# A two-layer GLA and Mamba-2 decoder step: scan outputs made by channels instead of by tokens

## The chip, the cores and the metric
One core of one Trainium2 chip runs the whole program. Five engines work in parallel, each through its own instructions in order: TensorE (PE, its weight loads shown as PEld), VectorE (DVE), ScalarE (ACT), GpSimd (POOL) and SyncE (SP), which issues most DMAs. The metric is the device time of one launch in microseconds, the median of three runs; less is better.

## The reference
Two layers over 1048 tokens: 8 samples of one token each, 16 meta tokens and 1024 prompt tokens. Layer 0 mixes by gated linear attention (GLA, 4 heads), layer 1 by Mamba-2 SSD (32 heads in 4 groups).
```python
for i in range(DEPTH):                       # x <- x + post(mixer(pre(x)))
    h = rmsnorm(x, pre_norm[i])
    y, S = gla_mixer(...) if i == 0 else ssd_mixer(...)
    x = x + rmsnorm(y, post_norm[i])
# GLA, per chunk
o = einsum('bhij,bjhv->bihv', attn, v) + einsum('bihk,bhkv->bihv', q * exp(bcum), S)
S = exp(b_last)[..., None] * S + einsum('bjhk,bjhv->bhkv', k_dec, v)
# then: o * rsqrt(mean(o*o) + EPS) * w_norm * silu(r), times w_out
# SSD, per chunk
y = einsum('bijg,bijgr,bjgrp->bigrp', cb, lmat * dt[:, None], x)
y = y + einsum('bign,bgrpn->bigrp', Cm, S) * exp(acum)[..., None]
S = exp(a_last)[..., None, None] * S + einsum('bjgn,bjgr,bjgrp->bgrpn', Bm, w, x)
# then: y + d_skip * x, times silu(z); rmsnorm over each group's 512 channels; times w_out
```

## The kernel before
Tokens are cut in 9 steps: step 0 has 24 tokens (samples and meta), steps 1 to 8 have 128 each. They form two groups (steps 0 to 4, steps 5 to 8), and the channels four units (a GLA head or an SSD group). An event is one unit at one step: 36 events per layer, 32 of 128 tokens.

The projection of a unit (L1257) is cut in pieces, 128 output channels by 268 or 512 tokens, each 24 products of fp32r high and low parts (weights w made by ACT L733 and DVE L747 from w_raw). It leaves channels in partitions and stores them to DRAM (kept_gq, kept_sq). The scan reads a chunk back per event: g_chunk (q, k, cumulative gate, v, v, r, r) or s_chunk (x in 4 tiles, B, C), and for the SSD s_decay (cumulative decay of 8 heads, laid over all partitions) and s_z (gate, 4 tiles).

`Plan` writes one order for all engines: `skeleton` lists an event's stages by name with an offset in events, and between them ("fill", x) lets in x shares of projection pieces, so that PE has work while the other engines prepare an event. Every engine runs its part of each stage in that order. When the last unit's projection is through, the fills are empty, and the last events of layer 1 stand bare. All products of plain f32 operands run as two records.

A GLA event: PE turns v and r (4 transposes, L1636), ACT copies them to vr_turned (L1648). PE makes the score levels (L1695, L1698, L1701), DVE merges them to g_attn (L1716). PE adds q x state (L1775, 128 tokens by 256 channels) and attention x v (L1792) in bank O, and makes the state's increment (L1776). DVE gates with r (L1799), ACT squares with a sum (L1810), POOL takes the root, PE turns o (2 transposes, L1818), ACT and DVE make its high and low parts (L1827, L1835), and PE multiplies by w_out (L718, helper `out_products`). ACT or DVE (L1882) scale by the root and add to y_acc.

An SSD event: PE turns x and B and multiplies B by C (L2066 to L2068). ACT makes decays (L2039 to L2051), DVE the masked and scaled operands (L2094 to L2108). `pe_scan`: C x state (L2191, one product of 512 columns in bank Y1), the state's increment (L2194 in bank SU), and for each of 8 heads the product inside the chunk (L2201: stationary decay 128x128, moving xdt of 64 columns). DVE updates the state and sums y (L2212 to L2234). PE turns z (4 transposes, L2243) into bank SU and DVE gates y by it (L2250). ACT squares with a sum (L2259); PE turns y (L2267) into SU; ACT makes s_yt_hi (L2276), DVE s_yt_lo (L2282); PE makes the output product (L718). As SU serves the state's increment and both turns, L2191's stage first waits until s_yt_lo is made (`banks_free`).

In step 0 each of the 8 samples has a state of its own. In the GLA each is multiplied by a stationary operand of 24 columns that is zero but for one (q_masked, L1742); in the SSD PE turns the sample's state (L2138), ACT copies it to s_ys (L2159), and L2148 multiplies it by c_masked in the same way, 512 columns wide; L2144 makes its increment.

Two lines that the words above rest on (L2191 and L2201):
```python
pe.matmul(self.Y[1][0:n, :], x[:, 5, :], self.S[:, u % 2, :], start=True, stop=True).then_inc(self.inter, 1)
last = pe.matmul(self.Y[0][0:n, r * HD:(r + 1) * HD], G[0:n, r, :], t["xdt"][0:n, r * HD:(r + 1) * HD],
                 start=True, stop=True)
```

## Time and profile before
| | us |
|---|---|
| three runs, median (lowest, highest) | 1708.35 (1705.63, 1716.34) |
| the profiled execution, its own time | 1704.04 |
| its span, first to last instruction | 1702.3 |
| PE busy | 1586.8 |
| DVE busy | 1212.3 |
| ACT busy | 805.9 |

The profile is of one execution, and numbers worked out from it are held against its own 1704.04 us, 4.3 us under the median. Busy times of PE overlap, as matmuls are pipelined; the distance between the starts of two rows of the timeline, divided by the first one's count, is its pace.

### The profile page before, as it was taken

The page shows a single profiled execution, that of the slowest core. Times are in us where ns is not written, and L with a number is a line of the kernel's source. Part 1 is how long each engine was busy: PE and PEld are TensorE (multiplying, and loading weights), DVE is VectorE, ACT ScalarE, POOL GpSimd, SP SyncE. Part 2 cuts the span into 40 slices and gives each one's busy share as a digit, 9 for nine tenths or more (in the row PEclk, how much of TensorE's full clock was granted, in tenths as well). Part 3 has the DMA queues.
Part 4 walks back from the last instruction along what each step waited for, and adds up shares of the span by engine and source line. Part 5 has one row for each costly group of instructions (what it writes and reads, how often), then busy time and mean ns, then how long its engine had stood idle before and what let it go on. Part 6 is the DMA issues. An engine that isn't in the chain of part 4 may idle for free. (4 is left out here: it accounts for less than half of the span.)

```text
span 1702.3 us, 26480 instructions
## 1 busy us (share of the span) xinstructions
PE 1586.8 (93%) x9274; PEld 1298.3 (76%) x9274; DVE 1212.3 (71%) x2351; ACT 805.9 (47%) x1738; POOL 228.7 (13%) x412
## 2 busy tenths in 40 slices
PE   6999999899999889979999999999999999999885
PEld 6879787667878778976788887787577778878764
DVE  4455487767877978867677678785677878587675
ACT  4634343355446454443553544444345455454451
POOL 4010112011211100112002002200201200000012
PEclk9999999999999999988999999999899999999998
DMA  5553446245565314455735564652465766665652
GB/s 166 149 153 108 134 137 173 62 122 161 159 208 172 111 47 124 147 162 172 176 91 155 160 165 136 185 133 65 144 173 144 196 175 158 162 159 134 165 128 80
DMA packets 313531, 244.80 MB, mean 144 GB/s; under 512 B 32773, under 2 KB 283465, under 8 KB 313369
## 3 DMA queue, kind: packets, MB, share of 16 engines
q1 hardware_dynamic: 305400, 216.90, 46.9%
q0 software_dynamic: 8000, 26.22, 5.0%
q8 instruction: 75, 1.23, 0.3%
q14 instruction: 56, 0.45, 0.1%
HBM read 182.59 MB, written 60.68 MB: 143 GB/s over the span
## 5 line engine op out<-in xcount | busy, mean ns | idle before, releaser
L1257 PE MATMUL bank<-h,w 128*128 128x268 f32 (+1 forms) x4752 | 841.8, 331 | 18.2 <-ACT w L733 15.7
L1257 PEld LDWEIGHTS bank<-h,w 128*128 128x128 f32 x4752 | 701.3, 191 | 122.5 <-issue 56.1
L718 PE MATMUL bank<-s_w_out,s_yt_hi 128*128 128x512 f32 (+1 forms) x576 | 182.7, 398 | 7.4 <-DVE s_ys L2234 3.2
L747 DVE TENSOR_TENSOR w<-w_raw,w 128x1024 fp32r<-128x1024 f32 x132 | 160.8, 1218 | 37.6 <-ACT w L733 37.3
L733 ACT ACTIVATE w<-w_raw 128x1024 fp32r<-128x1024 f32 x132 | 138.8, 1052 | 24.6 <-DMA w_raw<-in_ssd_w_in_dram 24.2
L1346 DVE SCALAR_TENSOR_TENSOR conv<-before_conv,cw,conv 128x260 f32<-128x260 f32 (+2 forms) x216 | 125.1, 579 | 6.8
L718 PEld LDWEIGHTS bank<-s_w_out,s_yt_hi 128*128 128x128 f32 (+1 forms) x576 | 101.0, 180 | 36.1 <-issue 4.4
L718 PE MATMUL bank<-s_w_out,s_yt_lo 128*128 128x512 f32 (+1 forms) x288 | 113.6, 394 | 0.0
L2019 POOL TENSOR_SCALAR s_ymean<-s_ysum 128x1 f32<-128x1 f32 (+1 forms) x36 | 17.2, 478 | 678.4 <-ACT squares L2259 678.4
L718 PE MATMUL bank<-g_w_out,g_ot_hi 128*128 128x512 f32 (+1 forms) x288 | 100.1, 430 | 1.9 <-DVE g_ot_lo L1835 1.9
L2044 ACT ACTIVATE s_decay<-s_decay,t_ac 128x128 f32<-128x128 f32 (+1 forms) x288 | 85.4, 378 | 1.2
L1716 DVE COPY_PREDICATED g_attn<-g_lmask,bank 128x128 f32<-128x128 int32 (+1 forms) x208 | 60.7, 292 | 29.4 <-PE bank L1698 21.3
L2201 PEld LDWEIGHTS bank<-s_xdt,s_decay 128*128 128x128 f32 (+1 forms) x576 | 66.8, 183 | 19.4 <-issue 19.4
L1301 ACT ACTIVATE conv<-bank,cw 128x268 f32<-128x268 f32 (+1 forms) x72 | 45.9, 638 | 72.1 <-PE bank L1257 65.8
L1558 POOL TENSOR_SCALAR g_omean<-g_osum 128x1 f32<-128x1 f32 (+1 forms) x36 | 16.2, 451 | 432.3 <-ACT squares L1810 432.3
L1386 DVE SCALAR_TENSOR_TENSOR stage<-stage,conv 128x268 f32<-128x268 f32 (+1 forms) x72 | 37.2, 517 | 48.1 <-ACT stage L1363 47.7
L2276 ACT ACTIVATE s_yt_hi<-bank 128x512 fp32r<-128x512 f32 (+1 forms) x36 | 20.1, 558 | 107.5 <-PE bank L2267 107.4
L718 PEld LDWEIGHTS bank<-g_w_out,g_ot_hi 128*128 128x128 f32 (+1 forms) x288 | 53.1, 187 | 19.4 <-DVE g_ot_lo L1835 4.0
L2201 PE MATMUL bank<-s_xdt,s_decay 128*128 128x64 f32 (+1 forms) x576 | 65.6, 267 | 0.0
L749 DVE SCALAR_TENSOR_TENSOR s_w_out<-w_raw,wn,s_w_out 128x1024 fp32r<-128x1024 f32 x32 | 40.9, 1281 | 32.6 <-ACT s_w_out L740 32.6
L740 ACT ACTIVATE s_w_out<-w_raw,wn 128x1024 fp32r<-128x1024 f32 x32 | 36.7, 1146 | 56.3 <-DMA w_raw<-in_ssd_w_out_dram 29.2
L718 PEld LDWEIGHTS bank<-s_w_out,s_yt_lo 128*128 128x128 f32 (+1 forms) x288 | 51.6, 179 | 15.0
(213 smaller groups left out, 2560.9 us busy)
## 6 DMA issues: line engine op xcount, KB each, us to landing
w_raw<-in_ssd_w_in_dram SPq DMA_DIRECT2D x80, 512.0 KB, 4.2
w_raw<-in_gla_w_in_dram SPq DMA_DIRECT2D x48, 512.0 KB, 4.3
s_decay<-kept_acd SPq DMA_DIRECT2D x32, 512.0 KB, 8.1
w_raw<-in_ssd_w_out_dram SPq DMA_DIRECT2D x32, 512.0 KB, 4.0
g_chunk<-kept_gq SPq DMA_DIRECT2D x32, 448.0 KB, 5.0
s_chunk<-kept_sq SPq DMA_DIRECT2D x32, 384.0 KB, 4.4
kept_sq<-stage SPq DMA_DIRECT2D x80, 134.0 KB, 4.4
kept_sq<-stage SPq DMA_DIRECT2D x40, 256.0 KB, 4.9
```

What stands on the lines that cost most here:

```text
L718: last = pe.matmul(bank[0:n, :], yt[a][:, k, 0:n], wo[:, k, b, 512 * half:512 * half + 512], start=(k + a + b == 0), stop=(k == tiles - 1 ...
L733: act.activation(self.part(i, 0), self.raw(i), ACT.Copy).then_inc(self.w_hi, 1)
L740: act.activation(self.part(i, 0), self.raw(i), ACT.Copy, scale=self.norm_column(w)).then_inc(self.w_hi, 1)
L747: dve.tensor_tensor(self.part(i, 1), self.raw(i), hi, ALU.subtract).then_inc(self.w_lo, 1)
L749: dve.scalar_tensor_tensor(out=self.part(i, 1), in0=self.raw(i), scalar=self.norm_column(w), in1=hi, op0=ALU.mult, op1=ALU.subtract).then_ ...
L1257: last = pe.matmul(bank[:, 0:n], w[:, p.tile % 2, a, k, :], h[:, b, k, c:c + n], start=(i == 0), stop=(i == len(terms) - 1))
L1301: act.activation(self.work(i)[:, 0:n], bank[:, 0:n], ACT.Identity, scale=m["cw"][:, 3, a:a + 1], bias=m["cw"][:, 4, a:a + 1])
L1346: ins = dve.scalar_tensor_tensor(out=u[:, off:n], in0=x[:, k:k + w], scalar=cw[:, k, a:a + 1], in1=u[:, off:n], op0=ALU.mult, op1=ALU.add)
L1386: dve.scalar_tensor_tensor(out=self.slot(i)[:, 0:n], in0=self.slot(i)[:, 0:n], scalar=1.0, in1=self.work(i)[:, 0:n], op0=ALU.add, op1=ALU. ...
L1716: dve.copy_predicated(g[:, :], mk[:, li, :].bitcast(I32), self.L[li // 4][0:n, (li % 4) * P:(li % 4) * P + n]).then_inc(self.attn_part, 1)
L2044: last = act.activation(L[0:n, r, :], L[0:n, r, :], ACT.Relu, scale=-1.0, bias=ac[0:n, s, h:h + 1])
L2201: last = pe.matmul(self.Y[0][0:n, r * HD:(r + 1) * HD], G[0:n, r, :], t["xdt"][0:n, r * HD:(r + 1) * HD], start=True, stop=True)
```

## The change
Both scans make their outputs with channels in partitions and tokens along the row, as the output product wants them.

In the SSD, C x state becomes 4 products (stationary a 128x128 piece of the state, moving C). The product inside the chunk has xdt (64 columns) as stationary and the decay matrix (128 columns) as moving operand, and writes even heads to partitions 0 to 63 and odd heads to 64 to 127. Skip, gate and halving read s_chunk and s_z as they lie; exp of the running sum is taken per head over all tokens (e_sum is now 4 tiles of 128). The turns of z and y are gone. ACT squares y in place once its low part is made; PE sums the squares over channels by 4 products with a column of ones (`pe_sum`, stage "sum"), ACT copies that column (`act_sum`, stage "root"), POOL takes the root as before.

In the GLA v alone is turned, r is used as it lies, q x state and attention x v are two products each of 128 channels, o is not turned, and its squares are summed in the same way. The state lies in states after even steps and in odd_state after odd ones. The chunk has three buffers instead of two.

Samples: the state (SSD: the turned one) is the stationary operand in pieces of 128, the sample's q or C the moving one, a single column; q_masked and c_masked are gone. Their GLA outputs are added by DVE in two small instructions per unit. s_z and conv_rows have one buffer instead of two; s_z is loaded by a stage of its own ("zload"), and conv_rows are stored one piece earlier.
```diff
         gla = [... ("turn", -1), ("fill", 0.5), ("load", 2),
-               ("fill", 0.5), ("samples", 0.4), ("state", 0), ("fill", 0.5), ("attend", 0), ("scale", 1),
+               ("sum", -1), ("fill", 0.5), ("root", -1), ("samples", 0.4), ("state", 0), ("fill", 0.5), ("attend", 0),
@@ ssd
-               ("weight", 3, 1), ("fill", 0.5), ("gates", 0), ("load", 2), ("lows",), ("fill", 0.3), ("norm", 0),
+               ("weight", 3, 1), ("fill", 0.5), ("load", 2), ("lows",), ("fill", 0.3), ("norm", 0), ("zload", 1),
...
-               ("fill", 0.3), ("lows",), ("weight", 2, 0), ("fill", 0.3), ("r_square", -1), ("r_out", -2), ("fill", 0.3)]
+               ("fill", 0.3), ("lows",), ("square", 0), ("weight", 2, 0), ("fill", 0.3), ("sum", 0), ("r_square", -1),
+               ("r_out", -2), ("fill", 0.3), ("root", 0)]
@@ Gla.pe_attend (state product moved here from pe_state)
+        for j in range(2):
+            out = self.O[:, j * P:j * P + n]
+            if s:
+                pe.matmul(out, self.state(u, s - 1)[:, j * P:(j + 1) * P], self.t["qe"][:, e % 2, 0:n], start=True,
+                          stop=False)
+            if j == 0:
+                pe.wait_ge(self.attn, e + 1)
+            last = pe.matmul(out, v[:, j * P:(j + 1) * P], g[:, :], start=(s == 0), stop=True)
@@ Ssd.load_gate, act_decay
+        if e:
+            sp.wait_ge(self.gated, e)
+        for i in range(2):
+            half = slice(HD * i, HD * i + HD)
+            act.activation(t["ea"][half, e % 2, :, 0:n], L[half].rearrange("p (t two) c -> p t two c", two=2)[:, :, i, :],
+                           ACT.Exp)
@@ Ssd.banks_free, pe_scan
-            pe.wait_ge(self.yt_lo, e)
-            pe.matmul(self.Y[1][0:n, :], x[:, 5, :], self.S[:, u % 2, :], start=True, stop=True).then_inc(self.inter, 1)
+            for j in range(4):
+                last = pe.matmul(self.Y[1][:, j * P:j * P + n], self.S[:, u % 2, j * P:(j + 1) * P], x[:, 5, :],
+                                 start=True, stop=True)
         for r in range(HPG):
-            last = pe.matmul(self.Y[0][0:n, r * HD:(r + 1) * HD], G[0:n, r, :], t["xdt"][0:n, r * HD:(r + 1) * HD],
+            at = slice(HD * (r % 2), HD * (r % 2) + HD)
+            last = pe.matmul(self.Y[0][at, (r // 2) * P:(r // 2) * P + n], t["xdt"][0:n, r * HD:(r + 1) * HD], G[0:n, r, :],
                              start=True, stop=True)
@@ Ssd: squares, sum and its copy
+        act.wait_ge(self.yt_lo, e + 1)
+        act.activation(y, y, ACT.Square).then_inc(self.rows.squared, 1)
+    def pe_sum(self, pe, u, s):
+        pe.wait_ge(self.rows.squared, self.rows.squares[("square", 1, u, s)])
+        pe.wait_ge(self.cb_masked, min(e + 2, len(EVENTS)))
+        for j in range(4):
+            last = pe.matmul(self.M[0:n, 2 * P:2 * P + 1], self.t["y"][:, j, 0:n], self.m["ones"][:, 0:1],
+                             start=(j == 0), stop=(j == 3))
+    def act_sum(self, act, u, s):
+        act.activation(self.t["ysum"][0:n, e % 4:e % 4 + 1], self.M[0:n, 2 * P:2 * P + 1],
+                       ACT.Copy).then_inc(self.sum_kept, 1)
```
PE, from the output product of one SSD event of group 1 to the next event's scan, before (ident is the unit matrix of a transpose, h,w a projection piece; the waits are semaphores by name):
```order
L2267 MATMUL bank<-ident,s_ys 128x128 [waits s_s_new,s_gated]
L2267 MATMUL bank<-ident,s_ys 128x128 x3
L1234 MATMUL bank<-ident,conv_cols 11x128 [waits piece_packed,piece_free0]
L1234 MATMUL bank<-ident,conv_cols 11x128
L1257 MATMUL bank<-h,w 128x512 [waits w_hi,piece_free1]
L1257 MATMUL bank<-h,w 128x512 x15
L1257 MATMUL bank<-h,w 128x512 [waits w_lo]
L1257 MATMUL bank<-h,w 128x512
L2191 MATMUL bank<-states,s_chunk 128x512 [waits s_s_new,s_yt_lo,s_y_summed,s_added]
L2194 MATMUL bank<-s_xw,s_b_turned 128x512 [waits s_b_turned,s_xw_ready]
L2201 MATMUL bank<-s_xdt,s_decay 128x64 [waits s_attn]
L2201 MATMUL bank<-s_xdt,s_decay 128x64 x7
```
And in the changed kernel:
```order
L1269 MATMUL bank<-h,w 128x512 x7
L1246 MATMUL bank<-ident,conv_cols 11x128 [waits piece_packed,piece_free0]
L1246 MATMUL bank<-ident,conv_cols 11x128
L1269 MATMUL bank<-h,w 128x512 [waits w_hi,piece_free1]
L1269 MATMUL bank<-h,w 128x512 x11
L2314 MATMUL bank<-ones,s_ys 128x1 [waits s_cb_masked,row_squared]
L2314 MATMUL bank<-ones,s_ys 128x1 x3
L1269 MATMUL bank<-h,w 128x512 x4
L1269 MATMUL bank<-h,w 128x512 [waits w_lo]
L1269 MATMUL bank<-h,w 128x512
L2233 MATMUL bank<-s_chunk,states 128x128 [waits s_s_new,s_y_summed,s_added]
L2233 MATMUL bank<-s_chunk,states 128x128 x3
```
The turns L2267 are gone, the sum L2314 stands some 12 projection products later and waits for the squares, and the state product, now L2233, no longer waits for s_yt_lo. Ahead of the first row stand 10 and 1 further projection products behind the output product in both.

PE in a GLA event of group 0, from the turn of o to the output product, before:
```order
L1818 MATMUL bank<-ident,g_o_gated 128x128 [waits g_vr_turned,g_o_gated]
L1818 MATMUL bank<-ident,g_o_gated 128x128
L1257 MATMUL bank<-h,w 128x268 x6
L1257 MATMUL bank<-h,w 128x268 [waits w_hi,piece_free0]
L1257 MATMUL bank<-h,w 128x268 x11
L1775 MATMUL bank<-states,g_q_inter 128x256 [waits row_squared,g_k_turned,g_o_gated,g_s_new,g_vr_turned,g_qi_ready]
L1776 MATMUL bank<-g_vr_turned,g_k_turned 128x256
L1257 MATMUL bank<-h,w 128x268 x4
L1257 MATMUL bank<-h,w 128x268 [waits w_lo]
L1257 MATMUL bank<-h,w 128x268
L1792 MATMUL bank<-g_vr_turned,g_attn 128x256 [waits g_attn]
```
And in the changed kernel:
```order
L1269 MATMUL bank<-h,w 128x268 x6
L1851 MATMUL bank<-ones,g_o_squares 128x1 [waits g_v_turned,row_squared]
L1851 MATMUL bank<-ones,g_o_squares 128x1
L1269 MATMUL bank<-h,w 128x268 x6
L1269 MATMUL bank<-h,w 128x268 [waits w_hi,piece_free1]
L1269 MATMUL bank<-h,w 128x268 x5
L1792 MATMUL bank<-g_v_turned,g_k_turned 128x256 [waits g_s_new,g_k_turned,g_v_turned]
L1269 MATMUL bank<-h,w 128x268 x6
L1815 MATMUL bank<-g_q_inter,g_odd_state 128x128 [waits g_o_gated,row_squared,g_v_turned,g_qi_ready]
L1819 MATMUL bank<-g_attn,g_v_turned 128x128 [waits g_attn]
L1815 MATMUL bank<-g_q_inter,g_odd_state 128x128
L1819 MATMUL bank<-g_attn,g_v_turned 128x128
```
The sum L1851 has come in behind six projection products, the two turns have gone, and q x state has moved from the state stage to the attention stage and is cut in two.

PE in the last unit of layer 1, where no pieces are left, before (from the end of an output product):
```order
L718 MATMUL bank<-s_w_out,s_yt_lo 128x512
L2267 MATMUL bank<-ident,s_ys 128x128 [waits s_s_new,s_gated]
L2267 MATMUL bank<-ident,s_ys 128x128 x3
L2191 MATMUL bank<-states,s_chunk 128x512 [waits s_s_new,s_yt_lo,s_y_summed,s_added]
L2194 MATMUL bank<-s_xw,s_b_turned 128x512 [waits s_b_turned,s_xw_ready]
L2201 MATMUL bank<-s_xdt,s_decay 128x64 [waits s_attn]
L2201 MATMUL bank<-s_xdt,s_decay 128x64 x7
L2243 MATMUL bank<-ident,s_z 128x128 [waits s_s_new,s_z_in1]
L2243 MATMUL bank<-ident,s_z 128x128 x3
L2066 MATMUL bank<-ident,s_chunk 128x128 [waits s_cb_masked,s_skipped,s_ck_in0]
```
And in the changed kernel:
```order
L724 MATMUL bank<-s_w_out,s_yt_lo 128x512
L2314 MATMUL bank<-ones,s_ys 128x1 [waits s_cb_masked,row_squared]
L2314 MATMUL bank<-ones,s_ys 128x1 x3
L2233 MATMUL bank<-s_chunk,states 128x128 [waits s_s_new,s_y_summed,s_added]
L2233 MATMUL bank<-s_chunk,states 128x128 x3
L2238 MATMUL bank<-s_xw,s_b_turned 128x512 [waits s_b_turned,s_xw_ready]
L2246 MATMUL bank<-s_decay,s_xdt 64x128 [waits s_attn]
L2246 MATMUL bank<-s_decay,s_xdt 64x128 x7
L2111 MATMUL bank<-ident,s_chunk 128x128 [waits s_cb_masked,s_sum_kept,s_xdt_ready,s_ck_in1]
```
The sum now stands directly behind the output product and ahead of the next event's scan.

## Rows read from the trace of the kernel before
**Rows 1.** The page's parts 1 and 2: busy time per engine; clock in 40 slices
```profile
PE 1586.8 (93%) x9274; PEld 1298.3 (76%) x9274; DVE 1212.3 (71%) x2351; ACT 805.9 (47%) x1738; POOL 228.7 (13%) x412
...
PEclk9999999999999999988999999999899999999998
```
**Rows 2.** Waits of PE up to 1550 us: us in total, times, longest
```profile
PE bank L1257 <- ACT w L733: 14.5, 9, 2.7
...
PE bank L2191 <- DVE s_yt_lo L2282: 4.6, 3, 3.8
PE bank L2243 <- DVE states L2216: 3.4, 3, 1.7
```
**Rows 3.** Waits of PE behind 1550 us
```profile
PE bank L2191 <- DVE s_yt_lo L2282: 7.9, 5, 2.9
PE bank L718 <- DVE s_ys L2234: 3.2, 4, 1.9
```
**Rows 4.** Timeline of PE, an event of the last unit: start us, us, what
```profile
1611.42 1.02 PE L2194 MATMUL bank<-s_xw,s_b_turned 128*128 128x512 f32 x2
1612.28 1.89 PE L2201 MATMUL bank<-s_xdt,s_decay 128*128 128x64 f32 x16
1614.01 0.61 PE L2243 MATMUL bank<-ident,s_z 128*128 128x128 f32 x4
1614.45 0.60 PE L2066 MATMUL bank<-ident,s_chunk 128*128 128x128 f32 x4
...
1615.84 0.70 PE L718 MATMUL bank<-s_w_out,s_yt_hi 128*128 128x512 f32 x2 [0.45 <-DVE s_ys L2234]
```
**Rows 5.** Timeline of PE, state products of a GLA event
```profile
506.59 0.59 PE L1775 MATMUL bank<-states,g_q_inter 128*128 128x256 f32 x2
507.02 0.59 PE L1776 MATMUL bank<-g_vr_turned,g_k_turned 128*128 128x256 f32 x2
```
**Rows 6.** Timeline of PE, levels of a GLA event
```profile
501.50 0.27 PE L1664 MATMUL bank<-ident,g_decays 128*128 128x128 f32 x1
501.70 0.51 PE L1695 MATMUL bank<-g_q_decayed,g_decays 128*64 128x64 f32 x6
502.14 1.38 PE L1698 MATMUL bank<-g_q_decayed,g_decays 128*128 128x128 f32 x10
503.36 0.39 PE L1701 MATMUL bank<-g_chunk 128*128 128x128 f32 x2
```
**Rows 7.** Groups of instructions by form: busy us, mean ns
```profile
L1257 PE MATMUL bank<-h,w 128*128 128x512 f32 x1584 | 403.1, 404 | 11.8 <-ACT w L733 11.8
...
L1108 PE MATMUL bank<-t_esum,ident 32*64 32x8 f32 x64 | 3.6, 250 | 0.0
...
L1695 PEld LDWEIGHTS bank<-g_q_decayed,g_decays 128*32 128x32 f32 x128 | 4.6, 108 | 2.2
...
L1882 DVE SCALAR_TENSOR_TENSOR y_acc<-bank,s_yrstd,y_acc 128x512 f32<-128x512 f32 x48 | 35.3, 746 | 29.5 <-PE bank L718 29.4
...
L2282 DVE TENSOR_TENSOR s_yt_lo<-bank,s_yt_hi 128x512 fp32r<-128x512 f32 x32 | 22.0, 688 | 17.1 <-ACT s_yt_hi L2276 17.0
...
L2276 ACT ACTIVATE s_yt_hi<-bank 128x512 fp32r<-128x512 f32 x32 | 19.1, 597 | 104.4 <-PE bank L2267 104.3
...
L2039 ACT ACTIVATE s_e_sum<-t_ac 128x8 f32<-128x8 f32 x32 | 6.4, 201 | 12.4 <-DMA s_decay<-kept_acd 12.4
```
**Rows 8.** Timeline of PE's weight loads, narrow stretch in rows 6
```profile
501.96 0.14 PEld L1695 LDWEIGHTS bank<-g_q_decayed,g_decays 128*32 128x32 f32 x4
```
**Rows 9.** Timeline of PE, one sample in the SSD
```profile
1051.45 1.04 PE L2148 MATMUL bank<-s_ys,s_c_masked 128*24 128x512 f32 x2
1052.42 1.74 PE L1257 MATMUL bank<-h,w 128*128 128x268 f32 x12
```
**Rows 10.** Windows: the last samples' stretch; busy us by engine, clock
```profile
1190.00:1206.00 16.00, 12.15 (x48) 8.18 (x46) 12.20 (x24) 4.32 (x9) 3.07 (x4) 0.68 0.48 152
```

More of the change, by code:

```diff
@@ L488, in _ @@
                 rows.root(pool, ("r", *at))
[L489 removed]
+            elif name == "root":
                 layers[at[0]].root(pool, *at[1:])
@@ L526, in _ @@
                 layers[at[0]].act_square(act, *at[1:])
+            elif name == "root":
+                layers[at[0]].act_sum(act, *at[1:])
             elif name == "turn":
@@ L596, in _ @@
                 ssd.pe_scan(pe, *at[1:])
-            elif name == "gates":
-                ssd.pe_gates(pe, *at[1:])
             elif name == "sample":
                 layers[at[0]].pe_sample(pe, *at[1:])
-            elif name == "turn":
-                layers[at[0]].pe_turn(pe, *at[1:])
+            elif name == "sum":
+                layers[at[0]].pe_sum(pe, *at[1:])
             elif name == "products":
@@ L1282, in act_evac @@
         elif p.kind == "tail":
-            if p.u or p.j == 2:
-                act.wait_ge(self.cv_stored, 128 * p.u + (64 if p.j == 2 else 0))
-            act.activation(m["cvo"][:, p.j % 2, :], bank[0:11, 0:2 * P], ACT.Copy).then_inc(self.free[i % 3], 1)
+            if p.u or p.j:
+                act.wait_ge(self.cv_stored, 128 * p.u + 32 * p.j)
+            act.activation(m["cvo"][:, :], bank[0:11, 0:2 * P], ACT.Copy).then_inc(self.free[i % 3], 1)
         elif p.kind == "plain":
@@ L1554, in root @@
         q = slice(e % 4, e % 4 + 1)
-        pool.wait_ge(self.rows.squared, self.rows.squares[("square", 0, u, s)])
+        pool.wait_ge(self.sum_kept, e + 1)
         if e >= 4:
@@ L1762, in dve_sample, with state @@
                                      op0=ALU.mult, op1=ALU.add).then_inc(self.ss_new, 1)
+    def state(self, u, s):
+        return self.t["odd"][:, :] if s % 2 else self.S[:, u, :]
     def pe_state(self, pe, u, s):
@@ L1797, in dve_gate @@
         if e:
-            dve.wait_ge(self.o_turned, e)
-        dve.tensor_tensor(t["og"][0:n, :], self.O[0:n, 0:HV], t["vr"][0:n, e % 2, HV:2 * HV],
+            dve.wait_ge(self.ot_hi, e)
+            dve.wait_ge(self.ot_lo, e)
+        if s == 0:
+            samples, own = self.output(NS), self.O[:, 2 * P:2 * P + 2 * NS].rearrange("p (t c) -> p t c", t=2)
+            dve.tensor_copy(t["os"][:, :, :], own).then_inc(self.with_states, 1)
+            dve.wait_ge(self.with_states, 2 * u + 1)
+            dve.tensor_tensor(samples, samples, t["os"][:, :, :], ALU.add).then_inc(self.with_states, 1)
+            dve.wait_ge(self.with_states, 2 * u + 2)
+        dve.tensor_tensor(t["og"][:, :, 0:n], self.output(n), self.tokens(u, s)[:, 5:7, :],
                           ALU.mult).then_inc(self.o_gated, 1)
@@ L2014, in root @@
         q = slice(e % 4, e % 4 + 1)
-        pool.wait_ge(self.rows.squared, self.rows.squares[("square", 1, u, s)])
+        pool.wait_ge(self.sum_kept, e + 1)
         if e >= 4:
@@ L2038, in act_decay @@
             act.wait_ge(self.y_summed, e - 1)
-        act.activation(t["ea"][0:n, e % 2, :], ac[0:n, s, HPG * u:HPG * u + HPG], ACT.Exp)
+        for i in range(2):
+            half = slice(HD * i, HD * i + HD)
+            act.activation(t["ea"][half, e % 2, :, 0:n], L[half].rearrange("p (t two) c -> p t two c", two=2)[:, :, i, :],
+                           ACT.Exp)
         act.activation(t["el"][:, e % 2, :].unsqueeze(2), L[:, :, n - 1:n], ACT.Exp).then_inc(self.el_done, 1)
@@ L2147, in pe_sample @@
         pe.wait_ge(self.ss_copied, i + 1)
-        pe.matmul(self.Y[1][0:n, :], t["cm"][:, b * C0:(b + 1) * C0], t["y"][:, :], start=(b == 0),
-                  stop=(b == NS - 1)).then_inc(self.inter if b == NS - 1 else self.ss_inter, 1)
+        for j in range(4):
+            last = pe.matmul(self.Y[1][:, j * P + b:j * P + b + 1], t["y"][:, j, :],
+                             self.tokens(u, 0)[:, 5, b:b + 1], start=True, stop=True)
+        last.then_inc(self.inter if b == NS - 1 else self.ss_inter, 1)
     def act_sample(self, act, u, b):
@@ L2153, in act_sample @@
         if b == 0 and e:
-            act.wait_ge(self.y_turned, e)
-            act.wait_ge(self.rows.squared, self.rows.squares[("square", 1, *EVENTS[e - 1])])
+            act.wait_ge(self.sum_done, e)
         act.wait_ge(self.ss_turned, NS * u + b + 1)
@@ L2172, in dve_sample, with tiles @@
             self.mask_b(dve, i + 1)
+    def tiles(self, bank, n):
+        return bank[:, :].rearrange("p (t c) -> p t c", t=4)[:, :, 0:n]
     def banks_free(self, pe, e):
@@ L2238, in pe_gates, with dve_gate @@
-    def pe_gates(self, pe, u, s):
+        dve.tensor_tensor(y[:, :, 0:c], y[:, :, 0:c], old, ALU.add).then_inc(self.y_summed, 1)
+    def dve_gate(self, dve, u, s):
         e, n = ev(u, s), step_cols(s)[1]
-        pe.wait_ge(self.z_in[e % 2], 16 * (e // 2 + 1))
-        pe.wait_ge(self.s_new, e + 1)
-        for j in range(4):
-            last = pe.transpose(self.SU[0:n, j * P:(j + 1) * P], self.t["zc"][:, e % 2, j, 0:n], self.m["ident"][:, :])
-        last.then_inc(self.z_turned, 1)
-    def dve_gate(self, dve, u, s):
-        e, n, y = ev(u, s), step_cols(s)[1], self.t["y"]
-        dve.wait_ge(self.z_turned, e + 1)
+        y = self.t["y"][:, :, 0:n]
+        dve.wait_ge(self.z_in, 16 * (e + 1))
```

275 lines of the change are left out of this document (134 added, 141 removed).

## The prediction
> **What bounds the kernel now.** I read the page first: TensorE (PE) is busy 93% of the span and VectorE (DVE) 71%, and the clock row stands at 9 in nearly every slice [rows 1]. So a microsecond taken off PE's work should come off the time, unless PE is standing there for somebody else. Second, PE's waits. They are short and scattered; those that bear on the change are 4.6 us before the state product L2191, for s_yt_lo, and 3.4 us before the turns of z, for the state, both up to 1550 us [rows 2]. Behind 1550 us the picture differs: there 7.9 us are waited in five stands for s_yt_lo, and 3.2 us for y itself [rows 3]. The program has run out of projection products there, and six events of the last unit stand bare. Third, the timeline, for the pace of PE. A busy time on PE overlaps its neighbours, so I take the distance from one start to the next, divided by the count.
>
> **The pace of PE.** An f32 product comes as two records, a transpose as one. Four transposes of 128x128 take 1614.01 to 1614.45, 0.11 us each [rows 4]. Two records of 512 columns take 0.86 us, 0.43 each [rows 4]; two of 256 take 0.43, 0.215 each [rows 5]; ten of 128 take 1.22, 0.12 each with a change of form among them [rows 6]. Sixteen records of only 64 columns (L2201) take 1.73 us, 0.108 each [rows 4]. That row is the key to this case: half the columns cost no less than all of them, so a record with a stationary operand 128 wide costs 0.11 us by its weight load, whatever it multiplies. A stationary operand of 64 with 8 columns has 3.6 us for 64 records, 0.056 [rows 7], again half for half the width.
>
> **The change part by part (PE's work).** An event is one unit's step; 36 per layer, 32 of 128 tokens and 4 of 24.
>
> Turns removed: z 144, y 144, o 72, r 72 transposes. Where 128 wide and long (384 of them) 0.11 each, the 24 of y's and o's that carry 24 tokens some 0.08, the 24 of z and r 0.11: 47 us less.
>
> Sums by a column of ones: per event 4 products in the SSD and 2 in the GLA, two records each, stationary 128 wide, one column. 384 full records at 0.11 are 42.2 us, 48 of 24 tokens at some 0.03 by their width are 1.4: 43.7 us more. So the turns that go are paid for almost wholly by the products that come. From below, at 0.056 a record, they are 22 us; from above 0.12 each, 47 us. I take 0.11, by the row of 64 columns.
>
> State and attention outputs cut in pieces of 128 columns: GLA 128 records of 0.215 (27.5 us) become 256 of 0.11 (28.2); SSD state products 64 of 0.43 (27.5) become 256 of 0.11 (28.2). 1.4 us more.
>
> The product inside the chunk (L2201, now L2246) swaps its operands: stationary 64 wide, moving 128, outputs in turns in partitions 0 to 63 and 64 to 127. If such neighbours run one behind the other, 16 records cost 16 x 0.11 = 1.76 us and two changes of form. The price of a change: from a transpose to L1695 0.20 us instead of 0.11, and six small records with a change inside take 0.44 us where by their widths (two at 0.056, four at 0.028) they would take 0.22 [rows 6], so 0.1 to 0.14 a change; two are 0.28. If the two halves run side by side, 8 x 0.11 + 0.28 = 1.16 us. The trace has such a pair: the four loads of the 32-wide forms of L1695, which go to two column groups, all start within 0.03 us and are over in 0.14 us, where a lone one takes 0.11 [rows 7, 8]. I take side by side: 1.73 less 1.16, 0.57 us less in each of 32 events, 18.2 us. The other end is 0.31 us more, 10 us more. The Trainium skill (TensorEngine Tiling, Key Properties) says both things: tiles in different columns load and multiply in parallel, and a change of tiling mode drains the engine. Of 64-wide pairs no run here shows it; the 32-wide pair of this trace agrees, with 0.14 us for four loads.
>
> Sample states: in the SSD the two records of 24x512 per sample take 0.97 us (1051.45 to 1052.42) [rows 9] and become 8 of one column at 0.11, 0.90; the form then changes once less, as the transposes before it and these products are both 128 wide: 0.12. 32 samples: 6 us less. In the GLA 64 records of 256 (13.8 us) become 128 of one column (14.1), and 16 changes of form go (1.9): 1.6 less.
>
> Sum of PE's work: -47.0 + 43.7 + 1.4 - 18.2 - 7.6 = -27.7 us.
>
> **Waits.** (a) The state product no longer waits for s_yt_lo, as y isn't turned in its bank, and the z turns that waited are gone: 4.6 + 3.4 = 8 us less up to 1550 us [rows 2]. What is late next there are the squares, but in 21 events PE has 4 to 8 us of work between the output product and the sum (counted in the changed order; in the place that the change's order rows show, 30 products of 512 columns at 0.25 [rows 7]), and the chain that has to fit is 2.6 us, so they are covered.
> (b) That chain: the output product ends, DVE adds its second half to y_acc (0.75), then y_lo (0.69), ACT squares (0.6, as its 128x512 copy), with three hops of some 0.15 [rows 7]: 2.6 us, in place of the waits before L2191 of 7.9/5 = 1.6 us [rows 3]. In the six bare events PE has nothing to cover it: 1.0 x 6 = 6 us more.
> (c) In the same six the gain on z and inside the chunk isn't had: the next output product waits for y_summed, which DVE ends after six operations in a row; PE already stands there, 3.2 us in four events [rows 3], and at 1615.84 it starts behind DVE, not behind its own work [rows 4]. 6 x (0.44 + 0.57) = 6 us given back.
> (d) Eight further events have only 1.4 to 2.8 us of products before the sum: some 0.3 us each, 2 us. The last event of each layer now has sum, copy and root behind the turn: 1 us each, 2 us.
> (e) ScalarE gets 36 x about 1.0 us: exp of the running sum is taken for all 128 tokens of 4 tiles by two instructions (64x512, each about 0.6 by the 128x512 row) in place of one of 0.20 [rows 7]. They stand one event ahead of need. What they can hurt are weights: PE waits 14.5 us for them today [rows 2]. I take 2 us; the bounds are 0 and 36.
> (f) The z load has one buffer and waits for the gate of the event before; SP issues it behind that gate and DVE is mostly its pacer, the load lands within an event of some 20 us: 0. conv_rows with one buffer: ACT waits for the store of the piece before, a few us off the path: 0 to 4, taken 0. VectorE loses some 8 us of narrower work in the four short events of each layer and is hidden: 0.
>
> Sum of waits: -8 + 6 + 6 + 2 + 2 + 2 = +10 us. All: -17.7, say -18. The profiled execution has 1704.04 us (its span 1702.3), so 1686; the median of the three runs lies 4.3 above it, so 1690.
>
> **Rivals.**
> 1. No side by side: the 64-wide halves take turns. 0.88 us more than forecast in the 26 events that aren't bare, 23: 1713. For it: the trace shows only 32-wide pairs. Against: [rows 8].
> 2. A one-column product hides its load and costs 0.056: 384 records of the sums and 384 of the samples at 0.054 less each, 41 us, 1649. For it: the 8-column row [rows 7]; against it: the 64-column row [rows 4], with the same width of load. The Trainium skill (TensorEngine Tiling, Instruction Overhead) gives about 60 cycles to any small product and tells nothing of the load; by it alone the sums and one-column products would cost even less than this rival's. The trace speaks against it with 0.108 us for 64 columns.
> 3. Slower: the chain to the sum becomes what PE waits for in every SSD event, not in the bare ones only, because ACT, now 1 us fuller per event, comes late to the squares, and PE stands in its order before the sum with the next state product behind it. Decides from the point at which the squares come more than the covering 4 to 8 us after the output product. With 2 us each in the 30 other events: 60 more, 1750; with half of it 1720. For: ACT and DVE take their work in a fixed order, and DVE is 71% busy. Against: ScalarE is 47% busy [rows 1], 36 us more make it 49%.
>
> **How the numbers follow.** Forecast as it stands, within 10 us: 0.47. Rival 1: 0.13. Rival 2: 0.06. Rival 3: 0.07. Rival 4: 0.08. Rival 5: 0.19. A measurement here can tell about 1% from no change, 17 us: below 1691 is faster, above 1725 slower. The forecast lies at that edge, so half of its share counts as faster (0.25), with rivals 2 and 5: 0.50 (rounded); slower 0.07 from rival 3 and 0.03 from 1 and 4 together: 0.10; the rest, 0.40, within 1%. Range 1664 to 1716: down beyond rival 5, up to 1 and the milder half of 4.
>
> **What would show it.** Records of L2246 in eight pairs, 1.1 to 1.3 us an event, not 1.9; sum products (L2314, L1851) at 0.11 a record; PE busy down by some 28 us; a wait of PE before L2314 of some 2.5 us in six events behind 1550 and none to speak of before; the wait before the output product in those six grown by about 1 us; ScalarE up by some 35 us. I am wrong if PE's work falls by less than 15 or by over 45 us, if L2314 waits in the middle of the layer, or if the time moves while PE's work doesn't.

## The result, and the profile after

The changed kernel is slower: 1798.32 us (median of four, 1794.35 to 1803.35) against 1712.34 (1705.63 to 1716.46) of the kernel before beside it, a ratio of 1.051 with a 95% interval of 1.0482 to 1.0539. The forecast was 1690, range 1664 to 1716. Here and below a median takes in every execution, while a ratio leaves out those in the slow state that some executions of any kernel show (a lower granted clock and a longer time).

The page after, where [rows 1] stands for the kernel before, and below it the line with the span and the mean granted clock:
```profile
PE 1647.2 (92%) x9858; PEld 1389.6 (78%) x9858; DVE 1205.1 (67%) x2350; ACT 838.8 (47%) x1776; POOL 215.0 (12%) x411
...
PEclk9999796989999998979997998999999999989987
```
```profile
core 0: 1792.6 us, clock 0.926
```
PE's busy time didn't fall by 28 us, it rose by 60. Its share of the span is still 92%, so by the busy shares nothing happened but more work. The clock row tells more: it had 9 nearly everywhere and now dips all along. TensorE's clock is granted at one of two levels, 2.4 and 1.2 GHz, so a mean of 0.926 over 1792.6 us is 2 x 0.074 x 1792.6 = 265 us at half clock. The kernel before had a mean of 0.976, 82 us by the same working. I call this the half-clock time.

On PE's side the 90 us by which the span grew are of two kinds. All its waits together are 101 us before and 131 after, 30 more (forecast: 10 more). The other 60 are busy time. As an estimate, if work takes twice as long at half clock, the 183 us of additional half-clock time cost some 92, so that the work at full clock fell by some 32, about as forecast (28).

PE's waits after (us in total, times, longest), which answer to [rows 2, 3]:
```profile
PE bank L2314 <- ACT s_ys L2307: 57.5, 30, 4.1
...
PE bank L1269 <- ACT w L739: 9.5, 6, 3.2
...
PE bank L724 <- DVE s_ys L2279: 5.7, 5, 1.7
```
The waits for s_yt_lo are gone, as forecast. In their place PE stands ahead of the SSD's sum of squares (L2314) in 30 events of 36, and this is now the longest wait by far. It splits into the events up to 1680 us, which have other products ahead of the sum, and the six bare ones behind 1680 us:
```profile
PE bank L2314 <- ACT s_ys L2307: 42.8, 24, 4.1
```
```profile
PE bank L2314 <- ACT s_ys L2307: 14.7, 6, 3.9
```
The event with the longest of these waits, in the timeline of all engines (start us, us, what, and in brackets the idle time and who ended it):
```profile
1057.45 4.60 PE L1269 MATMUL bank<-h,w 128*128 128x268 f32 x36
...
1058.19 1.22 DVE L2151 TENSOR_TENSOR s_decay<-s_decay,s_cb 128x1024 f32<-128x1024 f32 x1
...
1059.14 0.57 ACT L1313 ACTIVATE conv<-bank,cw 128x268 f32<-128x268 f32 x1 [4.92 <-PE bank L1269]
...
1059.94 0.44 ACT L1375 ACTIVATE stage<-conv 128x268 f32<-128x268 f32 x1
1060.26 0.64 ACT L2295 ACTIVATE s_yt_hi<-s_ys 128x512 fp32r<-128x512 f32 x1
1060.64 1.22 DVE L753 TENSOR_TENSOR w<-w_raw,w 128x1024 fp32r<-128x1024 f32 x1
...
1063.26 1.54 DVE L1358 SCALAR_TENSOR_TENSOR conv<-before_conv,cw,conv 128x260 f32<-128x260 f32 x3
1064.71 0.68 DVE L2300 TENSOR_TENSOR s_yt_lo<-s_ys,s_yt_hi 128x512 fp32r<-128x512 f32 x1
1065.43 0.63 ACT L2307 ACTIVATE s_ys<-s_ys 128x512 f32<-128x512 f32 x1 [4.53 <-DVE s_yt_lo L2300]
1066.11 1.14 PEld L2314 LDWEIGHTS bank<-ones,s_ys 128*128 128x128 f32 x5 [4.27 <-ACT s_ys L2307]
1066.11 1.23 PE L2314 MATMUL bank<-ones,s_ys 128*128 128x1 f32 x5 [4.06 <-ACT s_ys L2307]
```
Three engines come in turn. The output product is over at 1057.6, where the projection products (L1269) take over. On ACT, y_hi (L2295) stands in order behind four instructions of a piece, the first of which waited for PE until 1059.14, so it starts at 1060.26; y_lo (L2300) starts at 1064.71 behind pieces' work on DVE; the square (L2307) writes over y in place, so it has to wait for y_lo, which reads y. From the end of the output product to the sum it is 8.5 us, and PE had 4.6 us of projection products for it. In the other 23 of the 24 events the wait is shorter, 1.8 us in the mean of all, but of the same kind: the sum comes 2.2 to 12.4 us after the last output product's end (later still in the layer's first event, which has none just before it).

The other half of the story is in the GLA, where no such wait is. The first 40 us of a unit with samples, before and after (window, its length, busy us and records of PE, PEld, DVE, ACT, POOL, then granted clock, DMA share, GB/s):
```profile
180.00:220.00 40.00, 35.53 (x221) 26.62 (x220) 21.08 (x47) 13.90 (x27) 7.35 (x12) 1.00 0.51 156
```
```profile
180.00:220.00 40.00, 39.08 (x214) 33.16 (x213) 15.40 (x31) 10.11 (x19) 6.62 (x10) 0.74 0.33 101
```
PE is busier than before in it, and gets through fewer records (214, not 221), at a clock of 0.74 instead of 1.00. With 4.5 us of idle time in this stretch the kernel before kept its full clock, and with 0.9 us the changed one lost it.

What came as forecast is the product inside the chunk. In the timeline of PE after:
```profile
1340.18 1.09 PE L2246 MATMUL bank<-s_decay,s_xdt 128*64 128x128 f32 x16
1341.20 1.43 PE L1269 MATMUL bank<-h,w 128*128 128x512 f32 x5
```
Sixteen records take 1.02 us from start to start, against 1.73 in [rows 4].

### The profile page after: what moved, and what is told of

It is laid out like the page before. It is cut to its first block and busy times, and to the rows that moved or that the text cites. A ratio compares the mean times of both kernels' runs of the same rounds, so it can differ in the third digit from the quotient of the medians.

```text
span 1792.6 us, 27581 instructions
## 1 busy us (share of the span) xinstructions
PE 1647.2 (92%) x9858; PEld 1389.6 (78%) x9858; DVE 1205.1 (67%) x2350; ACT 838.8 (47%) x1776; POOL 215.0 (12%) x411
## 5 line engine op out<-in xcount | busy, mean ns | idle before, releaser
L1269 PE MATMUL bank<-h,w 128*128 128x268 f32 (+1 forms) x4752 | 871.4, 338 | 14.1 <-ACT w L739 9.5
L1269 PEld LDWEIGHTS bank<-h,w 128*128 128x128 f32 x4752 | 723.3, 197 | 100.3 <-issue 31.0
L2314 PE MATMUL bank<-ones,s_ys 128*128 128x1 f32 (+1 forms) x288 | 39.2, 257 | 57.5 <-ACT s_ys L2307 57.5
L2314 PEld LDWEIGHTS bank<-ones,s_ys 128*128 128x128 f32 (+1 forms) x288 | 37.2, 203 | 68.5 <-ACT s_ys L2307 67.9
L1922 DVE SCALAR_TENSOR_TENSOR y_acc<-bank,s_yrstd,y_acc 128x512 f32<-128x512 f32 (+1 forms) x54 | 39.7, 745 | 42.1 <-PE bank L724 42.1
L2256 DVE TENSOR_TENSOR states<-states,s_e_last 128x512 f32<-128x512 f32 x32 | 22.1, 691 | 67.6 <-PE bank L2233 67.5
L2197 ACT ACTIVATE s_ys<-bank 128x512 f32<-128x512 f32 x32 | 19.1, 597 | 100.7 <-PE bank L2175 100.7
```

The lines of the kernel that those rows point to most:

```text
L1269: last = pe.matmul(bank[:, 0:n], w[:, p.tile % 2, a, k, :], h[:, b, k, c:c + n], start=(i == 0), stop=(i == len(terms) - 1))
L1922: return dve.scalar_tensor_tensor(out=y, in0=bank, scalar=rstd, in1=y, op0=ALU.mult, op1=ALU.add)
L2314: last = pe.matmul(self.M[0:n, 2 * P:2 * P + 1], self.t["y"][:, j, 0:n], self.m["ones"][:, 0:1], start=(j == 0), stop=(j == 3))
```

## The experiments

Two theories stood at the start. The chain theory: PE waits for the squares, 57.5 us, and this is the loss. The clock theory: the products of one column (samples' states and sums) go with a fall of the granted clock, and this is the loss. All ratios are to the kernel before, which ran beside each run; "less than the changed kernel" is the difference of two such ratios, times 1710 us. "The right version" is the changed kernel with all three of the following edits and every output kept.

**Wide samples.** In both layers, and alike for the GLA's L1755:
```diff
-            last = pe.matmul(self.Y[1][:, j * P + b:j * P + b + 1], t["y"][:, j, :],
-                             self.tokens(u, 0)[:, 5, b:b + 1], start=True, stop=True)
+            last = pe.matmul(self.Y[1][:, j * P:(j + 1) * P], t["y"][:, j, :],
+                             ident[:, :], start=True, stop=True)
```

> The changed kernel, but each of the samples' state products (64 of GLA at L1755, 128 of SSD at L2186) moves 128 columns of the identity instead of one column; the weights, the count, the order and the waits stay (the samples' outputs are no longer the reference's). Chain theory (TensorE stands for ACT's squares ahead of 30 of the 36 SSD sums, 57.5 us in all; the clock is a consequence): nothing at the samples, the wait L2314 <- ACT s_ys stays at 55 to 60 us and the time within 5 us of 1798. If both hold, the samples give 30 to 45 us and the wait stays.

Measured: 1750.38 us, ratio 1.0251 (1.0213 to 1.0289), 44 us less than the changed kernel by the ratios. Mean clock 0.955, half-clock time 157 us, 108 less. The window from 180 to 220 us again, then the wait:
```profile
180.00:220.00 40.00, 35.51 (x228) 28.70 (x227) 22.71 (x51) 12.68 (x24) 7.34 (x12) 0.93 0.47 144
```
```profile
PE bank L2314 <- ACT s_ys L2307: 56.9, 30, 4.0
```
The products have 128 times the columns, and the stretch has most of its clock back and gets through more records. The wait is untouched. PE's waits in all stay too (131 and 129 us in the two profiles), and its busy time falls by 45. So the samples' products of one column cost 44 us by the clock, apart from the wait. In the two profiles 23 us of the gain lie in layer 0 (up to the first scan product of layer 1) and 25 in layer 1.

**Wide sums.** `self.M[0:n, 2 * P:3 * P]` with `ones[:, :]` in place of one column, and alike in the GLA.

> The changed kernel, but the sums of squares (L1851, L2314) move 128 columns of ones instead of one, and the first column is read: same results, same count, order and waits. If the cost of the sums is that they leave the array idle (clock theory, taken to its end): some 10 to 20 us less, above all behind 1400 us where half-clock stretches stand once in an event. If their cost is the stationary load, 0.11 us a record whatever moves (47 us in all), and the stand ahead of them (chain theory): no change, 0 to +10 us, and the wait at L2314 stays at 55 to 60 us.

Measured: 1775.63 us, ratio 1.0386 (1.034 to 1.0431), 21 us less; mean clock 0.946. This is at the upper end of the clock theory's figure, and the wait at L2314 stays (57.8 us). All of it is in layer 1: layer 0 took 771.8 us in the changed kernel's profile and 771.5 here.

**Squares apart.** The squares go to the tile that the row norms use, ahead of y_hi on ACT. As y is no longer overwritten, DVE and ACT may also write the next event's y once y_lo and the squares are made, where they waited for PE's sum before:
```diff
-        act.wait_ge(self.yt_lo, e + 1)
-        act.activation(y, y, ACT.Square).then_inc(self.rows.squared, 1)
+        act.wait_ge(self.gated, e + 1)
...
+        act.activation(self.tiles(self.m["junk"], n), self.t["y"][:, :, 0:n], ACT.Square).then_inc(self.rows.squared, 1)
```

> The changed kernel, but SSD's squares go to a tile of their own (the one that the row norms use for theirs), straight from the gated output and ahead of y_hi on ACT, so that they wait for neither y_hi nor y_lo; the sum stays where it is on TensorE. Chain theory: the wait of L2314 for ACT falls from 57.5 us to under 15, and the time by 35 to 60 us, to 1740 to 1765. Clock theory alone: the stands are filled by other stands and the time stays within 10 us of 1798; half-clock time of the samples' steps stays (GLA about 90 us). If both hold: -35 or more and the GLA part unchanged.

Measured: 1740.79 us, ratio 1.0155 (1.0098 to 1.0211), 61 us less. PE's longest wait is now another:
```profile
PE bank L1276 <- ACT w L740: 25.0, 13, 3.2
```
The wait at the sum is 1.8 us, and that for the weights, which ACT makes, was 9.5 us and is 25.0: 15 us have moved there. All of PE's waits together fell from 131 to 106 us only. That the time fell by about the whole 57.5 nonetheless is the clock's doing: PE's busy time fell by 26 us as well (1647.2 to 1621.3), and half-clock time by 53. The figure that the chain theory had was hit, but only half of it as time waited; the other half is work that ran at half clock before.

**All three.**

> All three edits together (wide samples' products, wide sums, squares apart and early). If chain and clock are separate causes that add, 70 to 100 us less than the changed kernel: 1700 to 1730. If only the chain counts: 1740 to 1765; if only the clock: 1755 to 1770.

(As in the first run, the samples' products move the unit matrix and not their q or C.) Measured: 1693.19 us, ratio 0.9912 (0.9883 to 0.9941), 102 us less than the changed kernel. The single gains sum to 126, so 24 us were counted twice. The single edits took 108, 75 and 53 us off the half-clock time, 236 in all, and together they take 160: a wait that goes and a product that widens save partly the same half-clock time. Its mean clock is 0.969.

**All three, with every result right.** Widening can keep every output. NM is 16; the 16 columns from the sample's own on are moved seven times over, and later samples overwrite the columns beyond it:
```diff
+            at = j * P + b
+            last = pe.matmul(self.Y[1][:, at:at + 7 * NM].rearrange("p (r c) -> p r c", r=7), t["y"][:, j, :],
+                             self.tokens(u, 0)[:, 5, b:b + NM].unsqueeze(1).to_broadcast([P, 7, NM]),
+                             start=True, stop=True)
```

> All three edits with every result kept: the samples' state products move 112 columns (the 16 columns from the sample's own on, seven times over) of which the first is kept, the sums move 128 columns of ones, SSD's squares are apart and early. Same count of records as the changed kernel. If the width alone is what counted in the two runs with wide products, the time is that of the run with all three edits, 1693 within 8 us, and below the kernel before (1708.6); if it was that a constant was moved instead of each sample's column (another tile read), 1740 as with squares apart alone.

Measured: 1697.53 us, ratio 0.9932 (0.9915 to 0.995). This beats both kernels: 5.5% under the changed one, and 0.7% under the one before, which is small but outside the interval. Its page:
```profile
PE 1575.8 (93%) x9858; PEld 1334.7 (79%) x9858; DVE 1204.1 (71%) x2350; ACT 835.8 (49%) x1776; POOL 219.1 (13%) x411
```
```profile
core 0: 1696.4 us, clock 0.971
```
As many records of PE as the changed kernel, each with as many columns or more, and 71 us less busy time.

**Before, with narrow products.** The clock theory from the other side: in the kernel before, L1742 and L2148 move one column instead of 256 and 512 (so the samples' outputs lack their states' part). Their stationary tile is 24 columns wide.
```diff
-        pe.matmul(self.Y[1][0:n, :], t["cm"][:, b * C0:(b + 1) * C0], t["y"][:, :], start=(b == 0),
+        pe.matmul(self.Y[1][0:n, 0:1], t["cm"][:, b * C0:(b + 1) * C0], t["y"][:, 0:1], start=(b == 0),
```

> The kernel before, with its samples' state products (GLA L1742, 256 columns moved; SSD L2148, 512) cut to one moving column (the samples' state outputs are left out). Work alone: L1742's 15.6 us and L2148's 33.5 us fall to about 7 us each, so 33 to 36 us less: 1672 to 1677. Clock theory (one-column products let the granted clock fall): half-clock time in the steps with samples rises above that of before, and at least a third of this is given back: 1685 to 1710.

Measured: 1704.71 us, ratio 0.9975 (0.9956 to 0.9993). By form, the product in the SSD (busy us, mean ns), in the kernel before and then in this one, and this one's clock and window:
```profile
L2148 PE MATMUL bank<-s_ys,s_c_masked 128*24 128x512 f32 x64 | 35.7, 642 | 5.6 <-ACT s_ys L2159 5.5
```
```profile
L2148 PE MATMUL bank<-s_ys,s_c_masked 128*24 128x1 f32 x64 | 6.8, 175 | 7.6 <-ACT s_ys L2159 7.4
```
```profile
core 0: 1702.4 us, clock 0.955
```
```profile
180.00:220.00 40.00, 34.30 (x178) 26.21 (x178) 19.19 (x46) 11.07 (x20) 6.63 (x10) 0.79 0.48 143
```
From start to start, L2148 went from 33.5 to 4.6 us and L1742 from 15.6 to 4.3, 40 us of work on the engine that is busy 93%. The time fell by 4. Half-clock time rose from 82 to 153 us, and in the window the clock went from 1.00 to 0.79 with no other edit. Not all of the 36 us between was the clock: PE's waits in all rose from 101 to 115 us, some 14. The rest went into the products around, which took longer (the projection products alone 13 us, waits left out). Layer 0 shows the clock best. It lost 11 us of products and got 13 us longer (749.2 to 762.4), with 5 us more of waits and half-clock time up from 27 to 82. Layer 1 lost 29 us of products and got 13 us shorter.

**Sums of one record.** As the right version, but with float32r squares and ones.

> As the run with all three edits and right results, but the squares are written and the ones kept as float32r, so that each sum is one record instead of two (216 instead of 432), 64 columns wide. If a record of a sum costs TensorE 0.11 us by its stationary load whatever else (so the sums' 47 us are a true price), 20 to 26 us less than that run: about 1670. If it is the chain or the clock that fills, 0 to 10 less.

Measured: 1700.01 us, ratio 0.9925 (0.9896 to 0.9955), so nothing was gained on the right version. Its sums by form, and its clock:
```profile
L2333 PE MATMUL bank<-round_ones,squares 128*128 128x64 f32 x128 | 17.5, 260 | 2.0 <-issue 2.0
```
```profile
core 0: 1700.4 us, clock 0.960
```
The records did halve, and from start to start the sums fell from 48 to 24 us. But half-clock time rose from 98 to 136, and PE's waits in all from 106 to 124 us, that for ACT's weights from 23.2 to 29.6 among them. So more of the saving went into waits than into the clock. The projection products alone, with the waits between them, went from 833 to 849 us, 8 of it waits. My expectation (20 to 26 us less) took the price of a record for the price in time, and missed; how the rest would split without the clock, no run shows.

**The heads in another order.** `for r in (0, 2, 4, 6, 1, 3, 5, 7)` at the chunk product, first on the changed kernel.

> The changed kernel with the 8 heads of the chunk product (L2246) issued in the order 0, 2, 4, 6, 1, 3, 5, 7 instead of 0 to 7: neighbours then write the same half of the partitions. Side by side theory (two products that write different halves of the partitions run at once, which took this product from 59.7 to 41.0 us in all): it goes back to 58 to 62 us and the time rises by 12 to 20 us to 1810 to 1818. Rival (the product is quicker since its stationary tile is 64 columns wide instead of 128): no change, 1798 within 5.

Measured: 1799.82 us, ratio 1.0508 (1.0476 to 1.054), the changed kernel's time and not the 12 to 20 us more that were expected. Its profile is of an execution of 1832.16 us, so the product's cost is read from a second run of the same edit:

> The changed kernel with the heads in the order 0, 2, 4, 6, 1, 3, 5, 7 once more, with more rounds and for a profile that is not disturbed: if the 16 us that the product loses cost nothing, 1798 within 5 and a stand at L2314 that is shorter by several us or half-clock time below 267 us; if the first four times hid a loss, 1808 or more.

Measured: 1817.31 us, ratio 1.0572 (1.0526 to 1.0617). The product takes 55.5 us from start to start, 14.5 more than in the changed kernel (41.0), and PE still waits 55.4 us at L2314. The two ratios lie 0.6% apart, so on this kernel the price of losing the side by side is, by the two, 0 or some 10 us. On the right version it is clearer.

> The run with all three edits and right results (1697.5), with the heads of the chunk product in the order 0, 2, 4, 6, 1, 3, 5, 7. The product itself goes from 41 to 57 us, as it did in the changed kernel, where the time did not follow. If that was because TensorE stood for the squares there anyway, the time follows here, where this stand is gone: +10 to +18, 1707 to 1716. If work on TensorE and half-clock time trade against each other everywhere (as the one-record sums suggest, 25 us of products less and no time less), the time stays within 5 of 1697.5, and half-clock time falls.

Measured: 1707.4 us, ratio 0.9983 (0.9968 to 0.9998), 0.5% or 9 us above the right version. The product in the right version, then here:
```profile
1273.78 1.09 PE L2258 MATMUL bank<-s_decay,s_xdt 128*64 128x128 f32 x16
1274.80 1.44 PE L1276 MATMUL bank<-h,w 128*128 128x512 f32 x5
```
```profile
1284.32 1.58 PE L2258 MATMUL bank<-s_decay,s_xdt 128*64 128x128 f32 x16
1285.83 1.44 PE L1276 MATMUL bank<-h,w 128*128 128x512 f32 x5
```
1.02 against 1.51 us with only the order changed: neighbours that write different halves of the partitions run side by side. It is not the 64-wide stationary tile, as that is the same in both. The tile (or the swap of the operands) has a smaller share: of the 0.71 us between 1.73 in [rows 4] and 1.02, 0.49 are the side by side, and 0.22 remain when it is lost. The Trainium skill (TensorE: Matmul & The Clock Gate, Measured speedup vs the span model) gives 2.38 times for three tiles of 32 columns side by side; the trace agrees that they overlap, with 1.5 times for two. In all it is 14.3 us of product (41.0 to 55.3), of which 9 show in the time.

**Which part of the third edit counts.** The right version, with the squares back where the changed kernel has them in ACT's order, and then directly behind y_hi:

> The run with all three edits and right results, but the squares stand where the changed kernel has them in ACT's order, behind y_hi, y_lo and one weight tile; only the tile of their own and the wait for the gated output instead of y_lo are kept. If the sum is late because the square waits for y_lo (the write over y in place), nearly all of the gain stays: 1695 to 1710. If it is late because the square stands late in ACT's order, the stand at the sum comes back, 40 us or more of it, and the time is 1735 to 1750.

> The same, with the squares right behind y_hi on ACT instead of ahead of it. y_hi waits for the last output product's reads, 74 us in 15 waits in the changed kernel; if that is what holds the square, the stand at the sum is back in those events, 10 to 20 us of it, 1705 to 1715. If not, the same time as with the squares ahead, 1697.5 within 5, and the 23 us in which the projections wait for ACT's weights (13 times) become fewer.

Measured: 1708.3 us, ratio 0.9981 (0.9964 to 0.9997) in the old place, 1697.53 us, ratio 0.9924 (0.9901 to 0.9947) behind y_hi. PE's wait for the squares in the old place, and behind y_hi:
```profile
PE bank L2329 <- ACT squares L2322: 35.0, 19, 4.1
```
```profile
PE bank L2329 <- ACT squares L2322: 9.8, 8, 2.3
```
In the old place the time is in the range of the first answer (the wait for y_lo), at its upper end, but 35 us of the wait come back, nearly what the second (the place) asked for, and 11 us show in the time. So the late place is one cause, and what the tile of its own frees is the larger one in time. That second part holds two things which no run takes apart: the square no longer waits for y_lo, and the next event's y no longer waits for the sum. Ahead of y_hi or behind it makes no difference to the time. I had thought that the waits for the weights would become fewer behind it; they didn't (25.5 us in 13 times).

## Why the prediction was wrong

**Step (a) of the waits failed.** It said that in 21 events PE has 4 to 8 us of products ahead of the sum, that the chain to the sum is 2.6 us, and that "they are covered". The cover was right (4.6 us in the event shown). The chain was not: 8.5 us there, and in the 24 events that wait and aren't bare it left PE 42.8 us of waits, where the sum had 2 (term (d)). I had summed three durations and three hops, as if ACT and DVE were free when their turn came. Both take their work in a fixed order with pieces' work between: y_hi started 2.6 us after the output product's end, and y_lo 3.8 us after y_hi's. In the six bare events ACT and DVE have no pieces to make, and there the same working held: five of them wait 2.2 us and one 3.9, 14.7 in all, where term (b) had 2.6 each. Rival 3 is this mechanism. It put 2 us on each of 30 events that aren't bare, 60 in all; measured are 1.8 us each in 24 of them, 42.8. The 57.5 us of the page are near its 60 by luck, as they hold the bare events too. I gave it 0.07 because ACT is busy only 47% and would be at 49% (it was at 47% of the longer span, and at 49% in the right version). A busy share tells nothing of how late an engine is in one chain that passes through it twice.

**The clock was no term of the sum, and rival 4 was too small.** This is the other step that failed: a cost put at nothing. Rival 4 named the cause and asked for slower stretches, but looked only at the SSD's four, at up to 8 us each, because a dip stood there already. The GLA's four starts, where the clock was 1.00 in the window shown, weren't counted at all. Runs: 44 us for the samples of both layers and 21 for the sums. Of the samples' part 25 us were in layer 1, within rival 4's 20 to 30; the 23 in layer 0 and the sums weren't in it.

**PE's work, term by term, from start to start.** The sums took 47.1 us (34.5 + 12.6) against 43.7 forecast, 0.109 us a record. Rival 2 (0.056) is out. The product inside the chunk went from 59.7 to 41.0, 18.7 less against 18.2; rival 1 is out. The state products in pieces (L2233) took 39.2 us in the changed kernel, but 28.8 in the right version, where 28.2 were forecast: the term was right at full clock and the clock spoilt it. The samples' products took 55.1 us (19.3 + 35.8) against 49.1 before, 6.0 more where about 2 less were forecast for them alone, and 48.4 with wide columns.

**What is left once both causes are taken away** is a kernel at 1693 (all three edits) or 1697.5 (with right results), 15 and 11 us under the kernel before. The sum had said 18. So the total of the other terms was about right, though its parts were so less well: the right version's profile has 11 us less of busy time than the kernel before (forecast 28) and 5 us more of waits (forecast 10), with half-clock time still 16 us longer. What was missing were two prices: 61 us for the late squares, and 65 for the narrow products (44 and 21). Less the 24 us that they share they are the 102 between the changed kernel and the one with all three edits. Rival 5 (hand-overs loosened, 1675) showed in no run.

**ScalarE** got 32.9 us more, against some 36. Term (e) put 2 us on PE's waits for the weights that ACT makes. In the changed kernel they fell (15.7 us in the whole kernel before, 9.5 after); they grew where the squares were moved forward (25.0 us, 25.5 right behind y_hi), and not in the old place (11.8).

**What stays open.** Why the clock falls with narrow products is not told by these runs, only that it does, in both directions. What the side by side is worth in the changed kernel itself is 0 or some 10 us by two runs. And the 61 us of the third edit are time waited and clock in about equal parts; why a wait that goes brings clock back was not tested apart.

## What to carry to other kernels

Price a chain between engines by the time at which each engine comes to its link in the order, read from the timeline, not by the durations of the links; and where a result is squared in place or otherwise used up, write the square to a tile of its own, so that this link doesn't wait for another reader. On a kernel that TensorE bounds, read the granted clock of every stretch that a change touches. Here the sums' products of one column with a full stationary tile took nearly as long as those of 128 columns (47.1 and 48.4 us), and all products of one column slowed what stood around them; giving them more columns made the kernel faster. And before a saving on TensorE is booked, ask whether the clock or a wait will take it back.

## What was not expected of the hardware

- Widening products from 1 to 128 moving columns made the kernel 44 us faster (samples) and 21 us faster (sums), with the same count of records.
- Narrowing them took 40 us of work off TensorE in the kernel before and 4 off the time, with 14 us more of waits; mean clock 0.976 to 0.955. Layer 0, with 11 us less of such work, got 13 us longer. Halving the sums' records in the right version took 24 us off and 0 off the time, with 17 us more of waits; 0.971 to 0.960.
- The clock falls without idle gaps: in the window 180 to 220 us of the changed kernel PE's records are busy 39.08 of 40 us, at a clock of 0.74. The Trainium skill (TensorE: Matmul & The Clock Gate, HAM oscillation) puts the fall in a thin matmul kernel down to gaps in which TensorE waits for a DMA. Here all gaps of the window together are under 1 us and the clock falls all the same, so a stretch without gaps is no proof of a full clock.
- Half-clock time costs less than half of its length. From the changed kernel to the one with wide samples it fell by 108 us and the time by 44, 0.4 us for each.
